# Triple mixer: the gate product stacked in fp32r, the decays cumulated by VectorE scans, the decayed keys turned by transposes

## What is computed

```python
g_f = log_sigmoid(gfl @ gla_gf_up[l] + gla_gf_bias[l]) / 16.0      # gfl: 256 x 16, gf_up: 16 x 256; g_b likewise
# gla_chunked, chunks of 64 tokens, once forwards and once on the flipped sequence
b = jnp.cumsum(g, axis=3)
qe, ke = q * jnp.exp(b), k * jnp.exp(-b)
k_end = k * jnp.exp(b_last - b)
a = where(tri, einsum('bhnid,bhnjd->bhnij', qe, ke), 0.0)
upd = einsum('bhncd,bhncv->bhndv', k_end, v)
# state = exp(b_last) * state + upd;  o = a @ v + qe @ state
```

## Time and profile before

| what | value |
|---|---|
| median of 3 runs | 2331.73 us (2331.3 to 2332.21) |
| span of the profiled execution | 2328.8 us |
| PE busy | 2318.0 us |
| DVE, ACT busy | 1681.3 us, 1256.9 us |

### The profile page before, as it was taken

The page is one execution under the profiler, slowest core; times in us unless marked ns, Lnnn a source line. Parts: engine busy times, 40 slices in busy tenths (PEclk is TensorE's granted clock), DMA queues, the critical chain, the costliest instruction groups (busy, mean ns, idle before and its releaser), DMA issues.

```text
span 2328.8 us, 32712 instructions
## 1 busy us (share of the span) xinstructions
PE 2318.0 (100%) x13658; PEld 2025.4 (87%) x13658; DVE 1681.3 (72%) x2141; ACT 1256.9 (54%) x1523; POOL 79.1 (3%) x116
## 2 busy tenths in 40 slices
PE   9999999999999999999999999999999999999999
PEld 8889889888888978888888877888888888788887
DVE  8867846875876788767766766687587667766873
ACT  6545664554554665545546754455455457554552
POOL 2000000000000020100010000001000100000000
PEclk9999999999999999999999999999999999999999
DMA  7655445565655426656655533566565555344654
GB/s 227 195 186 176 145 134 192 182 193 185 194 186 183 157 91 192 216 188 187 193 185 179 181 127 127 167 199 213 185 197 184 186 181 178 120 134 163 193 187 145
DMA packets 335043, 409.51 MB, mean 176 GB/s; under 512 B 7895, under 2 KB 285105, under 8 KB 334897
## 3 DMA queue, kind: packets, MB, share of 16 engines
q1 hardware_dynamic: 331632, 401.66, 53.8%
q0 software_dynamic: 3072, 5.69, 0.9%
q10 hardware_dynamic: 192, 0.08, 0.0%
HBM read 406.35 MB, written 1.05 MB: 175 GB/s over the span
## 4 chain that ended last, share of the span: by engine, by line
PE 94%; DVE 4%; ACT 1%; DMA 1%; issue 0%; POOL 0%; SPq 0%; DVEq 0%; POOLq 0%; ACTq 0%
PE bank L614 14%; PE acc L614 13%; PE bank L1382 11%; PE bank L622 7%; PE acc L622 7%; PE acc L706 6%; PE bank L706 6%; PE acc L693 4%; PE bank L713 3%; PE acc L713 3%; PE acc L790 3%; PE acc L2770 2%; PE acc L1552 2%; PE bank L3342 1%; PE bank L652 1%; PE bank L1331 1%
## 5 line engine op out<-in xcount | busy, mean ns | idle before, releaser
L504 DVE TENSOR_TENSOR part_lo<-raw,part_hi 128x2048 fp32r<-128x2048 f32 (+3 forms) x390 | 870.3, 2235 | 347.2 <-ACT part_hi L497 343.9
L497 ACT ACTIVATE part_hi<-raw 128x2048 fp32r<-128x2048 f32 (+3 forms) x390 | 728.5, 1868 | 335.0 <-DMA raw<-in_ffn_w 99.5
L614 PE MATMUL bank<-hT,part_hi 128*128 128x512 f32 x1408 | 328.2, 390 | 0.2 <-ACT part_hi L497 0.2
L614 PEld LDWEIGHTS bank<-hT,part_hi 128*128 128x128 f32 x1408 | 261.7, 188 | 53.2 <-ACT part_hi L497 0.4
L614 PE MATMUL acc<-hT,part_hi 128*128 128x512 f32 x1280 | 298.2, 390 | 0.0
L614 PEld LDWEIGHTS acc<-hT,part_hi 128*128 128x128 f32 x1280 | 237.7, 188 | 47.7
L1382 PE MATMUL bank<-part_hi,hT 128*128 128x512 f32 x768 | 247.3, 395 | 0.7 <-issue 0.7
L622 PE MATMUL bank<-hT,part_lo 128*128 128x256 f32 x1408 | 184.2, 284 | 0.0
L622 PEld LDWEIGHTS bank<-hT,part_lo 128*128 128x128 f32 x1408 | 178.1, 192 | 3.6
L1382 PEld LDWEIGHTS bank<-part_hi,hT 128*128 128x128 f32 x768 | 144.2, 188 | 32.8 <-issue 3.5
L622 PE MATMUL acc<-hT,part_lo 128*128 128x256 f32 x1280 | 166.4, 283 | 0.0
(11 more groups left out here) (547 smaller groups left out, 3291.9 us busy)
## 6 DMA issues: line engine op xcount, KB each, us to landing
raw<-in_ffn_w SPq DMA_DIRECT2D x122, 1024.0 KB, 5.3
raw<-in_w_in SPq DMA_DIRECT2D x48, 1024.0 KB, 5.0
raw<-in_ffn_w_up SPq DMA_DIRECT2D x44, 1024.0 KB, 5.4
raw<-in_ffn_w_gate SPq DMA_DIRECT2D x43, 1024.0 KB, 5.3
raw<-in_ffn_w_down SPq DMA_DIRECT2D x32, 1024.0 KB, 5.1
raw<-in_hy_w_in SPq DMA_DIRECT2D x22, 1024.0 KB, 5.0
raw<-in_ffn_w_down SPq DMA_DIRECT2D x16, 768.0 KB, 4.3
raw<-in_ffn_w SPq DMA_DIRECT2D x12, 768.0 KB, 4.5
```

What stands on the lines that cost most here:

```text
L497: t.e.activation(part_hi[:, n % SLOTS, 0:size], raw[:, n % SLOTS, 0:size], ACT.Copy).then_inc(hi_ready, 1)
L504: t.e.tensor_tensor(part_lo[:, n % SLOTS, 0:size], raw[:, n % SLOTS, 0:size], part_hi[:, n % SLOTS, 0:size].bitcast(F32), ALU.subtract).th ...
L614: mm = pe.matmul(tiles[:, f, :].rearrange("p (h s) -> p h s", h=2), slot_cols(s, 0)[:, k, f * P:(f + 1) * P], hT[:, :, k, :], start=(first ...
```

## The change

In words, for each pass and both directions d:

- Gate product. The weights and the gates are now split as weights of the pieces are: ACT rounds `gate_up` into rows 0 to 16 of a stacked tile `gate_s` and again into rows 32 to 47 (two copies, L3463 and L3464 of the changed kernel), DVE puts the rest of it into rows 64 to 80 (L3578); ACT rounds the flipped gates into rows 64 to 79 and 0 to 15 of `glx` (L3488, L3489), DVE their rest into rows 32 to 47 (L3590). One fp32r product over 96 rows then holds the three passes (L3367, four products of 96 rows by 256 columns). Its output has features on the partitions, tokens along the row. Both tiles are cleared by DVE at the mixer's start.
- Cumulation. DVE makes the log-decays right after the first `flip_out` (L3661), and four scans of 128 x 256 (L3669, backwards for d = 1) cumulate them with a restart at each chunk. The subtraction from the chunk's whole (L3688 and the lines by it) stands where the log-decays were made before.
- Exponentials. ACT takes the three exponentials of a direction in `fill(6)` and `fill(8)` as before, now out of SBUF.
- Decayed keys. DVE multiplies them by the keys feature-major in `fill(7)` and `fill(9)` (L2989), PE transposes them in `fill(8)` and `fill(10)` (L2854, four transposes each), ACT copies them out (`ke_out`, L2916). The two multiplications in `grow` are gone, and so are all of L2851 and L2856.

The core of the diff:

```diff
         def na_tensor(t, l, pair):
             def fill(i):
-                if i == 6:
-                    t.banks.skip(2)
-                if i in (6, 8):
-                    d, incl, rest = ((0, C_LE, C_GT), (1, C_GE, C_LT))[i // 2 - 3]
-                    b = claim(t)
-                    for j in range(2):
-                        for a in range(TT):
-                            mm = pe.matmul(bank[:, b, j * S + a * P:j * S + (a + 1) * P], gg[:, d, a, j * P:(j + 1) * P],
-                                           late(incl, P), start=True, stop=True)
-                    mm.then_inc(full[b], 1)
+                if i in (8, 10):
+                    d = i // 2 - 4
+                    pe.wait_ge(gla_kf, t.see(gla_kf))
                     b = claim(t)
                     for a in range(TT):
-                        mm = pe.matmul(bank[:, b, a * 256:(a + 1) * 256], late(rest, P), gg[:, d, a, :],
-                                       start=True, stop=True)
+                        for j in range(2):
+                            o = (2 * a + j) * P
+                            mm = pe.transpose(bank[:, b, o:o + P], kf[:, d, j * S + a * P:j * S + (a + 1) * P], ident)
                     mm.then_inc(full[b], 1)
+                    ke_made.append(evicted(t, b))
         def na_scalar(t, l, pair):
                 if i in (6, 8):
                     d = i // 2 - 3
-                    b = filled(t)
-                    act.activation(ep[:, d, :, :], bank_of(b).rearrange("p (j s) -> p j s", j=2), ACT.Exp, scale=tau)
-                    act.activation(em[:, d, :, :], bank_of(b).rearrange("p (j s) -> p j s", j=2), ACT.Exp, scale=-tau)\
-                        .then_inc(taken[b], 1)
-                    b = filled(t)
-                    act.activation(ke[:, d, :, :], bank_of(b).rearrange("p (a n) -> p a n", a=TT), ACT.Exp, scale=tau)\
-                        .then_inc(taken[b], 1)
+                    sums_of = gsum[:, d, :].rearrange("p (j s) -> p j s", j=2)
+                    act.wait_ge(gla_sums, l + 1)
+                    act.activation(kf[:, d, :], kf[:, d, :], ACT.Exp, scale=tau)
+                    act.activation(ep[:, d, :, :], sums_of, ACT.Exp, scale=tau)
+                    act.activation(em[:, d, :, :], sums_of, ACT.Exp, scale=-tau).then_inc(gla_exp, 1)
+                if i == 9:
+                    ke_out(0)
+            ke_out(1)
             gate_scalar(t, 1, pair)
         def na_vector(t, l):
+                if i in (7, 9):
+                    d = i // 2 - 3
+                    dve.wait_ge(gla_exp, t.see(gla_exp))
+                    v = kf[:, d, :].rearrange("p (j s) -> p j s", j=2)
+                    dve.tensor_tensor(v, v, gkT[:, :, :], ALU.mult).then_inc(gla_kf, 1)
         def triple_tensor(t, l):
-            pe.wait_ge(gl_flipped, t.see(gl_flipped))
+            pe.wait_ge(gl_low, t.see(gl_low))
             for d in range(2):
-                for a in range(TT):
-                    mm = pe.matmul(acc[:, 2 + d, a * 256:(a + 1) * 256], gl_rows[:, d, a * P:(a + 1) * P], gate_up[:, d, :],
+                for j in range(2):
+                    mm = pe.matmul(acc[:, 2 + d, j * S:(j + 1) * S], gate_s[:, d, j * P:(j + 1) * P], glx[:, d, :],
                                    start=True, stop=True)
         def triple_scalar(t, l):
             next_hi(t)
             next_hi(t)
+            act.wait_ge(later_in, later_loaded(l))
+            act.wait_ge(gate_room, l + 1)
+            act.activation(gate_s[0:17, :, :], gate_up[0:17, :, :], ACT.Copy).then_inc(gate_hi, 1)
+            act.activation(gate_s[32:48, :, :], gate_up[0:16, :, :], ACT.Copy)
             act.wait_ge(root_col_ready, t.see(root_col_ready))
         def triple_vector(t, l):
-            t.link(dve.memset(gl_rows, 1.0))
+            dve.memset(glx[:, :, :].bitcast(F32), 1.0)
+            dve.memset(gate_s[:, :, :].bitcast(F32), 0.0).then_inc(gate_room, 1)
             dve.wait_ge(later_in, later_loaded(l))
+            dve.wait_ge(gate_hi, l + 1)
+            dve.tensor_tensor(gate_s[64:81, :, :], gate_up[0:17, :, :], gate_s[0:17, :, :].bitcast(F32), ALU.subtract)
             flip_out(t, lqT, 4, gain[:, G_MQ + l:G_MQ + l + 1], P, 1)
+            dve.wait_ge(gl_log, t.see(gl_log))
+            for d in range(2):
+                ins = dve.scalar_tensor_tensor(ge[:, d, :], g_raw[:, d, :], 0.0, ge[:, d, :], ALU.min, ALU.subtract)
+            t.done(ins, gl_decays)
+            for d in range(2):
+                for j in range(2):
...
+                    ins = dve.tensor_tensor_scan(sum_of, restart, g_of, 0.0, ALU.mult, ALU.add)
+            t.link(ins)
```

More of the change, by code:

```diff
@@ L138, in constants @@
     same = i // GLA_C == j // GLA_C
-    for at, m in ((C_LE, i <= j), (C_GT, i > j), (C_GE, i >= j), (C_LT, i < j)):
+    for at, m in ((C_LE, i <= j), (C_GT, i > j)):
         c[:, at:at + P] = same & m
+    c[:, C_CHUNK:C_CHUNK + S] = key % GLA_C != 0
     half = MLA_R // 2
@@ L325, in two_blocks @@
             lkT = sb("lkT", [P, MLA_H, S], where=m)
+            with ExitStack() as g:
+                glx = sb("glx", [GATE_ROWS, 2, S], F32R, where=g)
+                gate_s = sb("gate_s", [GATE_ROWS, 2, 256], F32R, where=g)
             lqrT = sb("lqrT", [P, 2, S], where=m)
@@ L2835, in na_tensor @@
             base, pairs = NA_H * l, NA_H // 2 * l
-            last = None
+            last, ke_made = None, []
             lo = lambda h: 64 * (h % 2)
@@ L2913, in na_scalar, with ke_out @@
             tau = 1.0 / 16.0
+            def ke_out(d):
+                b = filled(t)
+                act.activation(ke[:, d, :, :], bank_of(b).rearrange("p (a n) -> p a n", a=TT), ACT.Copy)\
+                    .then_inc(taken[b], 1)
             def fill(i):
@@ L2981, in fill @@
                     dve.tensor_copy(gkT[:, :, :], bank_of(b).rearrange("p (j s) -> p j s", j=2)).then_inc(taken[b], 1)
[L2982 to L2985, removed]
+                if i in (7, 9):
[3 more added lines that the diff above has]
+                    dve.tensor_tensor(v, v, gkT[:, :, :], ALU.mult).then_inc(gla_kf, 1)
+                if i in (8, 10):
+                    t.banks.take()
                 if i in (3, 7):
@@ L3405, in triple_tensor @@
                 pe.wait_ge(*b)
-            na_tensor(t, l, pair)
-            mla_tensor(t, l, gla_tensor(t, l))
+            ke_made = na_tensor(t, l, pair)
+            mla_tensor(t, l, gla_tensor(t, l, ke_made))
             banks = []
@@ L3481, in triple_scalar @@
             act.wait_ge(gl_flip, t.see(gl_flip))
-            act.activation(glT[:, :, :], acc[0:16, 1, :].rearrange("p (d s) -> p d s", d=2), ACT.Copy)\
-                .then_inc(gl_flipped, 1)
+            gl = acc[0:16, 1, :].rearrange("p (d s) -> p d s", d=2)
+            act.activation(glx[64:80, :, :], gl, ACT.Copy)
+            act.activation(glx[0:16, :, :], gl, ACT.Copy).then_inc(gl_flipped, 1)
             next_hi(t)
@@ L3518, in triple_scalar @@
             act.wait_ge(gl_in, t.see(gl_in))
-            t.link(act.activation(ge[:, :, :, :], g_raw, ACT.Abs))
-            t.link(act.activation(ge[:, :, :, :], ge[:, :, :, :], ACT.Exp, scale=-1.0))
-            act.activation(ge[:, :, :, :], ge[:, :, :, :], ACT.Ln, bias=1.0).then_inc(gl_log, 1)
+            t.link(act.activation(ge[:, :, :], g_raw, ACT.Abs))
+            t.link(act.activation(ge[:, :, :], ge[:, :, :], ACT.Exp, scale=-1.0))
+            act.activation(ge[:, :, :], ge[:, :, :], ACT.Ln, bias=1.0).then_inc(gl_log, 1)
             pair = take_pair(t)
@@ L3646, in triple_vector @@
             flip_out(t, lqT, 4, gain[:, G_MQ + l:G_MQ + l + 1], P, 1)
+            dve.wait_ge(gl_log, t.see(gl_log))
+            for d in range(2):
+                ins = dve.scalar_tensor_tensor(ge[:, d, :], g_raw[:, d, :], 0.0, ge[:, d, :], ALU.min, ALU.subtract)
+            t.done(ins, gl_decays)
+            restart = late(C_CHUNK, S)
+            for d in range(2):
+                for j in range(2):
+                    g_of, sum_of = (v[:, d, j * S:(j + 1) * S] for v in (ge, gsum))
+                    if d:
+                        g_of, sum_of = g_of[:, ::-1], sum_of[:, ::-1]
+                    ins = dve.tensor_tensor_scan(sum_of, restart, g_of, 0.0, ALU.mult, ALU.add)
+            t.link(ins)
             t.banks.skip(2)
@@ L3660, in triple_vector @@
             next_lo(t)
[L3661 removed]
             for d in range(2):
[L3663 to L3665 removed]
+                of_chunks = gsum[:, d, :].rearrange("p (n s) -> p n s", s=GLA_C)
+                whole = of_chunks[:, :, (GLA_C - 1, 0)[d]:(GLA_C, 1)[d]].to_broadcast([P, 2 * S // GLA_C, GLA_C])
+                ins = dve.tensor_tensor(kf[:, d, :].rearrange("p (n s) -> p n s", s=GLA_C), whole, of_chunks, ALU.subtract)
+            ins.then_inc(gla_sums, 1)
             take_pair(t)
```

46 lines of the change are left out of this document (19 added, 27 removed).

## The result

The changed kernel takes 2338.42 us (median of 12 executions, 2333.7 to 2339.89), the kernel before, on the same chip, 2331.75 us (12 executions, 2330.5 to 2332.92). The ratio of the means is 1.0024, 95% interval 1.0016 to 1.0032: slower by more than 0.2% at the middle. In the medians it is slower by 6.7 us (1.0029); means and medians differ since the executions fall into two groups. The forecast was 2335.2, its range 2330.0 to 2340.0.

What follows compares the result with a forecast made beforehand. PE, busy for 2318.0 of 2328.8 us, was taken as the bound. Opening, gate product and attention summed to +1.9 us in the first pass and +1.65 in the second, together +3.5: 2335.2 us, range 2330.0 to 2340.0.

Steps and rivals of the forecast that it cites:

- The opening: Before the query pair's first product, PE waits for DVE's low part, delayed by the gate-weight split: +2.1 and +1.85 us.
- the gate product: Ahead of the latent projections, four fp32r matmuls replace eight float32 ones on PE: -1.5 us a pass.
- the attention: Cumulation and decayed keys on PE: 3.8 us leave, 1.0 of transposes and two waits come, +1.3 us a pass.
- The keys' wait: At the start of `fill(8)`, PE waits for DVE's multiplication of the decayed keys: 3.6 us a pass.
- The bank claim: With `fill(6)` empty, PE waits for ACT's tanh evictions to free two banks: 0.4 us a pass.
- Log-decays and scans: Moved ahead on DVE into 4.91 us of idle time; scans 0.7 us each, 4.1 us together, costing nothing.
- two signs of being wrong: PE's waits in the two passes summing to under 8 us, or waits showing at L3379, would refute the prediction.
- rival A: The forecast itself: both new PE waits, in opening and attention, as worked out; 2333 to 2337.5 us, chance 0.60.
- rival C: Clock drops to half behind the wait for decayed keys: +1.9 us a pass, 2339.0 us, chance 0.15.
- Rival D: Pieces behind the opening come late and PE waits at latent projections: up to +1.5 a pass, 2338.2 us, chance 0.17.
- Rival B: No wait for decayed keys in `fill(8)`: 2327.9 us, or 2323.9 without the opening's wait too; chance 0.08.
- a slice lower: Sign that the prediction is wrong: the profile's clock row for PE shows a slice below full clock.

Runs made afterwards that it cites:

- both: Changed kernel with the gate product and its splitting moved later, and the decayed keys' transposes moved to i = 10 and behind the loop: 2329.19 us, ratio 0.999.
- bare wait: Kernel before, with only a DVE copy of the GLA keys onto themselves that PE waits for at i = 8: 2339.73 us, ratio 1.0038.

## Why the prediction was right and wrong

**Right: every term of the sum.** The opening +2.0 (forecast +2.1 and +1.85), the gate product -1.45 (-1.5), the attention +1.1 (+1.3). The keys' wait was 3.3 us and not 3.6: ACT's copy began 0.81 us after the start of the transposes and not 0.96, the chain behind it took 3.02 us and not 3.11, and the profile counts the wait only from the end of the transposes. (The terms that the prediction adds up for this part give +1.2; its +1.3 follows from its start times for L2902.) The bank claim cost 0.44 us (1362.16 to 1363.01, against 0.41 from start to start in the earlier trace rows), as forecast. Log-decays and scans were hidden, with scans of 0.61 us for an estimated 0.7. Of the two signs of being wrong that can be read off the waits, neither came: they sum to 10.3 us, and none shows at L3379. But the sum is that of an execution at full clock. The median, 2338.42, lies outside rival A's 2333 to 2337.5; it is in the range only because that was drawn to hold most of C and D as well. Slower by over 0.2%, which came, had a chance of 0.35.

**Rival D** (pieces late behind the opening) had nothing in it: the next stretch changed by +0.13 and -0.04 us. **Rival B** was no alternative even where both waits are away: "both" gave 2329.2 where B without the opening's wait had 2323.9, since B took the whole -2.8 of the attention and the whole -1.5 of the gate product, of which 0.5 each were left. The first number overlooked that the products removed from `fill(8)` were the cover of the softmax chain. Filled again with work that was ready, 1.9 of the 2.8 came.

**Wrong: the weighing of A against C.** The step that failed is the sentence of rival C that the clock "never fell", and its condition, that it "decides from a wait longer than the trace has and only behind the keys' wait", with a chance of 0.15. The executions of the changed kernel went C's way in 7 of 12, and the median is theirs. Two things in it were wrong, and its number came out in part by luck.

- The clock row gives tenths of 58 us slices, so a few microseconds at half speed don't show in it. Windows of 20 us over the trace of before do show a fall, in the mixer of the earlier trace rows, behind waits of 1.36 and 0.98 us (7 of the 11 profiles have one there):

```profile
820.00:840.00 20.00, 16.98 (x127) 12.59 (x127) 18.04 (x69) 13.52 (x47) 11.33 (x20) 0.91 0.21 71
```

  Nor would the sign I named, a slice lower, have shown it: that row is all nines after the change, too. In the changed kernel the mean clock of each execution shows it, 0.999 and 1.000 against 0.996 and 0.997; a single short fall it hides as well (0.999 in the profile of before).
- It is not the keys' wait alone. Falls came behind the opening's wait as well (1.5 to 1.6 us each, in three profiles, behind 2.0 to 2.3 us), and behind the keys' wait cut to 2.2 us.
- The price per fall, forecast at +1.9, lies within the measured 1.35 to 2.8 us. But C's 2339.0 had two falls behind the keys' waits; the profiled execution of the second group had one of 1.6 us behind the opening and one of 2.6 us behind the keys.

The Trainium skill's rule ("TensorE: Matmul & The Clock Gate", "HAM oscillation"), that gaps let the gate throttle PE again, is borne out: the bare wait did it with all of PE's work unchanged. Not every gap does it, though: the same kernel with the same 3.3 us waits ran at 1.00 in one profile and at 0.51 in another.

**Open:** what decides in an execution whether the clock falls behind a wait of 2 to 3.3 us. No run here controlled it. That the groups come from these falls is shown for the two profiled executions; of the others only the mean clock is known, which agrees.

## What to carry to other kernels

On an engine that is busy without a gap, a product that is removed may be the cover of another engine's chain; before removing it, ask what the next product waits for, and what ready work can take its place. A new wait on TensorE costs its length, and waits of 2.0 to 3.3 us cost here, in some executions, another 1.35 to 2.8 us from the clock; so read the granted clock in narrow windows and for each execution, and don't take a row of nines as proof. Price the opening and the inside of a stage apart: here the idea was sound, and moving steps of it, with every product as in the changed kernel, turned a loss of 6.7 us into a gain of 7.4.

## What the runs showed of the hardware

- The granted clock fell to half (0.50, 0.51: 1.2 GHz) behind waits of PE of 2.0 to 3.3 us, not each time, and behind two waits of 1.36 and 0.98 us close together. It stayed there for some 3 to 7 us and came back while PE went on with its work. One fall cost 1.35 to 2.8 us.
- Four fp32r products of 96 rows by 256 columns, three precision passes stacked on the rows, took 0.48 us (1271.82 to 1272.30) where eight float32 matmuls of 17 rows by 256 took 1.92 (1268.48 to 1270.40 in the earlier trace rows).
- A scan of 128 x 256 float32 on DVE took 0.61 us, one of 16 x 128 took 0.41 us: twice the columns and eight times the partitions for half as much time again.
